# Low parts of the 42 projection weight units stored by the first block and loaded by the other three

## The reference

```
mod  = silu(c) @ W_ada + b_ada                    # shift, scale, gate for both halves
h    = rms_norm(x) * (1 + scale1) + shift1
proj = h @ W_in                                   # q,k,v | deltanet q,k,v | beta,decay | z | gate A | gate B
oA   = sliding_window_attention(...)              # window 128, sinks, QK norm, partial rope
oD   = gated_deltanet(causal_conv(qkv), ...)      # chunks, a triangular inverse per chunk
x    = x + gate1 * ((sigmoid(gA) * (oA @ Wb_A) + sigmoid(gB) * (oD @ Wb_B)) @ W_out)
x    = x + gate2 * swiglu(rms_norm(x) * (1 + scale2) + shift2)
```

## Time and profile before

| | |
|---|---|
| median of 3 runs | 2879.8 us (2879.57 to 2880.38) |
| the profiled execution's own time | 2879.23 us |
| its span | 2877.3 us |
| granted TensorE clock, mean | 0.995 |
| PE busy | 2830.7 us (98%) |
| DVE busy | 1815.7 us (63%) |
| ACT busy | 1239.3 us (43%) |
| DMA traffic | 523.51 MB, mean 182 GB/s |

### The profile page before, as it was taken

The page is one execution under the profiler, slowest core; times in us unless marked ns, Lnnn a source line. Parts: engine busy times, 40 slices in busy tenths (PEclk is TensorE's granted clock), DMA queues, the critical chain, the costliest instruction groups (busy, mean ns, idle before and its releaser), DMA issues.

```text
span 2877.3 us, 39886 instructions
## 1 busy us (share of the span) xinstructions
PE 2830.7 (98%) x14954; PEld 2331.7 (81%) x14954; DVE 1815.7 (63%) x3122; ACT 1239.3 (43%) x2232; POOL 133.3 (5%) x124
## 2 busy tenths in 40 slices
PE   8999999999999999999999999999999999999999
PEld 6887888977877888888889877788778888888887
DVE  5876576875687666658876666665757622223686
ACT  4654545554444333334445554365544311112343
POOL 0011000010020000000000110000100100000000
PEclk9999999999999999999999999999999999999999
DMA  7443354533448787886433334424243676777743
GB/s 289 157 147 107 121 165 132 187 95 115 142 165 311 291 296 291 298 332 207 140 116 111 120 94 136 154 82 156 78 140 121 218 242 232 245 245 264 299 136 102
DMA packets 222512, 523.51 MB, mean 182 GB/s; under 512 B 43249, under 2 KB 43505, under 8 KB 213361
## 3 DMA queue, kind: packets, MB, share of 16 engines
q1 hardware_dynamic: 173056, 423.39, 44.8%
q10 hardware_dynamic: 49264, 97.57, 8.9%
HBM read 362.03 MB, written 158.86 MB: 181 GB/s over the span
## 4 chain that ended last, share of the span: by engine, by line
PE 85%; DVE 7%; ACT 3%; DMA 2%; DVEq 2%; issue 1%; SPq 1%; POOL 0%; ACTq 0%
PE gb L2457 26%; PE mb L2501 22%; PE gb L2501 19%; PE gb L2882 5%; PE gb L2487 4%; PE mb L2726 2%; PE mb L2699 1%; PE mb L2721 1%; PE mb L2627 1%; ACT sc L1364 1%; DVE tmp_c L2068 1%; DVE w_lo L1616 1%; DVE inv_c L2071 1%; PE mb L2792 1%; DVE a_mx L2052 1%
## 5 line engine op out<-in xcount | busy, mean ns | idle before, releaser
L2457 PE MATMUL gb<-h_hi,w_hi 128*128 128x512 f32 x1024 | 408.2, 399 | 4.1 <-DVE w_lo L1616 3.5
L2457 PE MATMUL gb<-h_lo,w_hi 128*128 128x512 f32 x1024 | 406.2, 397 | 0.0
L2457 PE MATMUL gb<-h_hi,w_lo 128*128 128x512 f32 x1024 | 406.2, 397 | 0.0
L2501 PE MATMUL mb<-t_hi,fw_both 128*128 128x512 f32 x1056 | 349.9, 393 | 9.2 <-DVE t_lo L1794 5.1
L1616 DVE TENSOR_TENSOR w_lo<-w_raw,w_hi 128x1024 fp32r<-128x1024 f32 x216 | 262.7, 1219 | 80.1 <-ACT w_hi L1074 79.1
L1074 ACT ACTIVATE w_hi<-w_raw 128x1024 fp32r<-128x1024 f32 x216 | 227.9, 1055 | 87.7 <-PE gb L2882 40.9
L2501 PEld LDWEIGHTS mb<-t_hi,fw_both 128*128 128x128 f32 x1056 | 199.9, 189 | 54.5 <-DVE t_lo L1794 7.8
L2457 PEld LDWEIGHTS gb<-h_hi,w_hi 128*128 128x128 f32 x1024 | 192.9, 188 | 53.2 <-issue 7.3
L2457 PEld LDWEIGHTS gb<-h_lo,w_hi 128*128 128x128 f32 x1024 | 193.1, 189 | 42.8 <-issue 5.3
L2457 PEld LDWEIGHTS gb<-h_hi,w_lo 128*128 128x128 f32 x1024 | 192.9, 188 | 40.3
L2501 PE MATMUL gb<-td_hi,fw_both 128*128 128x512 f32 x704 | 219.7, 390 | 0.3 <-DVE td_lo L1783 0.2
(11 more groups left out here) (370 smaller groups left out, 5966.2 us busy)
## 6 DMA issues: line engine op xcount, KB each, us to landing
w_raw<-in_wstream SPq DMA_DIRECT2D x216, 512.0 KB, 3.6
scratch_parts<-fw_both ACTq DMA_DIRECT2D x154, 512.0 KB, 4.1
fw_both<-scratch_parts SPq DMA_DIRECT2D x154, 512.0 KB, 4.7
scratch_hid<-spill SPq DMA_DIRECT2D x22, 1792.0 KB, 7.4
td_raw<-scratch_hid SPq DMA_DIRECT2D x154, 256.0 KB, 3.0
ada_buf<-in_ada_w SPq DMA_DIRECT2D x24, 1024.0 KB, 7.7
w_raw<-in_wgate SPq DMA_DIRECT2D x34, 512.0 KB, 8.2
wq<-in_wdown SPq DMA_DIRECT2D x8, 1280.0 KB, 11.3
```

The costliest lines, as they stand in the source:

```text
L2457: last = pe.matmul(bank(j), w, r, start=(i == 0), stop=(i == n - 1))
L2501: done = pe.matmul(out, w, (lo if part == 1 else hi)[:, tile, :] if tile is not None else (lo if part == 1 else hi), start=(first and part ...
```

## The change

In block 0, units 12 to 53 are split as before, and ACT stores each one's `w_lo` to memory (`park_u`), two splits later. DVE waits for the store to land before it writes that slot's `w_lo` again. In blocks 1 to 3, DVE does not split these 42 units: ACT's `split` issues a DMA on its own queue that loads `w_lo` from memory into the slot, ahead of the high-part copy, and PE waits for the high part and for the landing. Units 0 to 11 of each block are split as before. SP's raw loads wait for the high part where the unit before in the slot is a kept one. Semaphores with an early use that is over are reused for the counts.

```diff
+def is_kept(g):
+    return g >= U_PER and g % U_PER >= U_AT
+def splits_to(g):
+    return sum(not is_kept(i) for i in range(g + 1))
+KEPT_PER_SLOT = (U_PER - U_AT) // RING
...
+    park_u = nc.dram_tensor("scratch_units", (U_PER - U_AT, P, UW), fp32, kind="Internal").ap()
...
             def load_unit(b, u):
-                sp.wait_ge(w_ready.sem, b * U_PER + (u + 1))
+                if is_kept(g - RING):
+                    sp.wait_ge(w_high.sem, w_high.at(0, g - RING + 1))
+                else:
+                    sp.wait_ge(w_ready.sem, w_ready.at(0, splits_to(g - RING)))
...
             def split(b, u):                      # ACT
+                unit_used(b, u - RING)
+                if is_kept(b * U_PER + u):
+                    if b == 1 and u == U_AT:
+                        for last in range(U_PER - RING, U_PER):
+                            act.wait_ge(*store_landed(last))
+                    act.dma_start(w_lo[s][:, :].bitcast(fp32), park_u[u - U_AT]).then_inc(kept_landed(b, u)[0], 16)
                 act.wait_ge(w_loaded[s], 16 * ((b * U_PER + u) // RING + 1))
-                unit_used(b, u - RING)
...
                 act.activation(w_hi[s][:, :], w_raw[s][:, :], ACT.Copy).then_inc(w_high.sem, 1)
+                if U_AT + 2 <= b * U_PER + u < U_PER + 2:
+                    store_unit(b * U_PER + u - 2)
+            def store_unit(g):
+                s = g % RING
+                act.wait_ge(w_ready.sem, w_ready.at(0, splits_to(g)))
+                act.dma_start(park_u[g - U_AT], w_lo[s][:, :].bitcast(fp32)).then_inc(unit_out[s].sem, 16)
...
             def split(b, u):                      # DVE
-                dve.wait_ge(w_high.sem, b * U_PER + (u + 1))
+                g = b * U_PER + u
+                if is_kept(g):
+                    return
+                dve.wait_ge(w_high.sem, w_high.at(0, g + 1))
+                if U_AT <= g - RING < U_PER:
+                    dve.wait_ge(*store_landed(g - RING))
...
+            def parts_there(b, u):                # PE
+                g = b * U_PER + u
+                if is_kept(g):
+                    pe.wait_ge(w_high.sem, w_high.at(0, g + 1))
+                    pe.wait_ge(*kept_landed(b, u))
+                else:
+                    pe.wait_ge(w_ready.sem, w_ready.at(0, splits_to(g)))
...
-                    pe.wait_ge(w_ready.sem, w_ready.at(b, u + 1))
+                    parts_there(b, u)
```

More of the change, by code:

```diff
@@ L152 @@
 LAST_USE, HALVES = last_uses()
+def is_kept(g):
[3 more added lines that the diff above has]
+KEPT_PER_SLOT = (U_PER - U_AT) // RING
+assert U_AT % RING == 0
 ADA_FIRST, ADA_TURNS = 4, 12
@@ L608, in layer_program, with kept_landed @@
     uses = [[n for n in range(N_GATE) if part_slot(1, n) == k] for k in range(PARTS)]
-    per_raw = [16 * (slots[k] + len(uses[k])) for k in range(6)]
-    f_loaded = [Signal(raw_in[k], per_raw[k]) for k in range(4)]
-    t_loaded = [Signal(raw_in[k], per_raw[k], gate_loads[k]) for k in range(6)]
-    parts_in = [Signal(raw_in[k], 0, gate_loads[k] + 16 * slots[k]) for k in range(6)]
+    unit_in = [KEPT_PER_SLOT * 16 if k >= 4 else 0 for k in range(6)]
+    per_raw = [16 * (slots[k] + len(uses[k])) + 2 * unit_in[k] for k in range(6)]
+    f_loaded = [Signal(raw_in[k], per_raw[k], unit_in[k]) for k in range(4)]
+    t_loaded = [Signal(raw_in[k], per_raw[k], unit_in[k] + gate_loads[k]) for k in range(6)]
+    parts_in = [Signal(raw_in[k], 0, 3 * unit_in[k] + gate_loads[k] + 16 * slots[k]) for k in range(6)]
+    def kept_landed(b, u):
+        k = (5, 4, None)[slot(b, u)]
+        n = (b - 1) * KEPT_PER_SLOT * 16 + 16 * ((u - U_AT) // RING + 1)
+        if k is None:
+            return sin_done, 2 + n
+        return raw_in[k], n + (gate_loads[k] + 16 * slots[k] if b >= 2 else 0)
     t_high, t_ready = sig("t_high", N_DOWN_STEPS), sig("t_ready", N_DOWN_STEPS)
@@ L634, in layer_program, with store_landed @@
     spilled = Signal(zeroed, 16 * NPAIR, 16 * 2 * NT)
+    unit_out = [Signal(sem, 0, 1) for sem in (c_silu, picks_set, picks_summed)]
     parts_out = [Signal(sem, 0, before) for sem, before in (
-        (c_silu, 1), (ada_kept, len(ADA_ROWS)), (nea_exp, 1), (picks_set, 1), (picks_summed, 1), (ada_rows, len(ADA_ROWS)))]
+        (c_silu, 1 + KEPT_PER_SLOT * 16), (ada_kept, len(ADA_ROWS)), (nea_exp, 1), (picks_set, 1 + KEPT_PER_SLOT * 16),
+        (picks_summed, 1 + KEPT_PER_SLOT * 16), (ada_rows, len(ADA_ROWS)))]
+    def store_landed(u):
+        return unit_out[u % RING].sem, unit_out[u % RING].at(0, 16 * ((u - U_AT) // RING + 1))
     def parts_count(n):
@@ L683, in load_unit @@
             def load_unit(b, u):
-                sp.wait_ge(w_ready.sem, b * U_PER + (u + 1))
-                s = slot(b, u)
+                g, s = b * U_PER + u, slot(b, u)
+                if is_kept(g - RING):
+                    sp.wait_ge(w_high.sem, w_high.at(0, g - RING + 1))
+                else:
+                    sp.wait_ge(w_ready.sem, w_ready.at(0, splits_to(g - RING)))
                 sp.dma_start(w_raw[s][:, :], wstream[UNITS[b * U_PER + u][0]]).then_inc(w_loaded[s], 16)
@@ L840, in _ @@
                             if v < 3:
-                                sp.wait_ge(w_ready.sem, w_ready.at(b, U_OUT + 6 + v))
+                                sp.wait_ge(w_high.sem, w_high.at(b, U_OUT + 6 + v))
                             elif v == 3:
```

## The result

The changed kernel takes 2887.5 us, the median of 19 runs (2878.9 to 2892.4), beside 2880.4 for the kernel before (19 runs, 2875.6 to 2884.0). The ratio is 1.0024, with a 95% interval of 1.0018 to 1.0031. The change makes the kernel slower by 0.24%; forecast was 0.12% faster, and the time lies 6 us above the range. Two later executions of the kernel before, of 3160.6 and 4003.8 us at clocks of 0.84 and 0.65, are left out of every ratio.

What follows compares the result with a forecast made beforehand. PE was taken as the bound, busy 2830.7 of 2877.3 us, so only its waits could shrink. 2879.23 - 6.8 (stops gone) + 2.3 (OUT+1) + 1.2 (block 0) = 2875.9; forecast for the median 2876.5 us, range 2870.5 to 2881.5.

Steps and rivals of the forecast that it cites:

- What bounds the kernel: Whole kernel: PE, busy 2830.7 of 2877.3 us, is the bound; only PE's waits in blocks 1 to 3 can be won.
- The inverse ends 3.5 us sooner: Blocks 1 to 3: three splits fewer on DVE end the inverse 3.5 us sooner and move the `lc_u` load forward.
- the one limit that I saw: Block 1: DVE's step at 621.27 needs ACT's copy, so it can start 1.15 us sooner instead of 1.22.
- I take about half, 1.0 us: Image DMAs: cost of a 512 KB unit load sharing from another queue, about half of 2.1 us.
- the margin of block 2: Worst block's `lc_u` stop: 3.5 - 1.9 - 0.6 = 1.0 us left before PE would wait for the image again.
- The images gain nothing: Rival, chance 0.22: unit loads and stores interleave with the image DMAs, 4.1 us less gain, 2880.6 us.
- Block 0, 1.2 us more: Block 0's `lc_u` stop: GATE+7's store stands with the image writes and adds 1.2 us, ends 0 and 4.2.
- OUT+1, 2.3 us more: Unit OUT+1, blocks 1 to 3: low part's load, issued after ACT's second square, lands 0.75 us later each, 2.3 in all.
- OUT+1 late: Rival, chance 0.11: OUT+1's low part lands at 8.3 us beside the raw load and `x`, costing 14 us: 2890.6.
- faster by over 0.2%: Outcome given 0.25: the rival that all stops of blocks 1 to 3 go (2868.9 us, 0.13) plus the forecast's lower edge.
- `w_lo` 1.7: Blocks 1 to 3, units GATE+8 and GATE+9: PE's stops for DVE's low part go, gain 1.7 us.
- `t_o` 0.6: PE's stop for `t_o` stays almost whole, since POOL's root limits it; gain 0.2 us a block, 0.6 in all.

Runs made afterwards that it cites:

- The second move: The change with only GATE+10's low-part load and GATE+8's store issued after the images' read back; 2874.0 us, 0.9979 of the kernel before.

## Why the prediction was wrong, step by step

- **What bounds the kernel**: right as far as it went. PE is busy 98% before and after, and the lighter DVE gained nothing as long as the images' way was not clear. But only PE's standing still was counted as what could be won or lost. The level of the clock behind a stop was no term, put at nothing without a reason: 2.7 us between the two traces, and about 5 of the 7 between the medians, by the estimate above.
- **The inverse ends 3.5 us sooner**: 2.76, 2.6 and 2.6. Two splits gone left DVE waiting for ACT again (0.24 and 0.40 us in the rows above) instead of the one limit that I saw.
- **"I take about half, 1.0 us"** for one neighbour, "which fits in the margin of block 2 and leaves something over": the failed term. The size was nearly right, 0.9 on the writes and 1.2 on the landing, but there are two neighbours, one on each half of the chain, and they add up to 2.1. The margin was too wide too, since the inverse gave 2.6 to 2.76, and PE comes 1.4 to 1.75 us sooner, not 0.6. Instead of 4.1 us gained, the stops in blocks 1 to 3 went from 4.5 to 7.1.
- **The images gain nothing**, the rival with 0.22, was the right mechanism and still too mild: it let the stops stay as they were and left out both PE's earlier arrival and the clock.
- **Block 0, 1.2 us more**: 2.0 measured (1.7 to 3.7), inside the ends of 0 and 4.2. That nothing else is waited for there was right.
- **OUT+1, 2.3 us more**: 1.1. The stops were to be 1.3, 1.0 and 1.0 us, 2.3 above those for `w_lo` that they replace; they are 0.7 three times, 2.1 in place of 1.0. The load landed in 3.25 us, not 3.6, and PE comes to it 0.4 us later behind ACT's second square than before:

```profile
775.14 0.33 ACTq L1108 DMA_DIRECT2D w_lo<-scratch_units  x1
...
778.48 0.47 PE L2517 MATMUL gb<-mg_hi,w_hi 128*128 128x512 f32 x1 [0.67 <-issue]
```

- **OUT+1 late**, the rival with 0.11, did not happen, although the load of `x` behind it took 12 us to land: it was issued 2.0 us after.
- **The chances**: 0.25 for "faster by over 0.2%" takes 0.12 from a forecast whose own range, 2873.5 to 2879, lies below 2874.0 for only half a us; that share is too large by the prediction's own numbers.
- **`w_lo` 1.7, `st_vr` 0.4, `t_o` 0.6, issues and waits 0, `a_mx` and `sc` 0**: 1.7 (the other 1.0 of the 2.7 is OUT+1's), 0.4, 0.4, and nothing new in the waits. Right.
- **The sum**: forecast -3.3 us. The stops of the two traces changed by +4.6 (`lc_u`: 2.6 in blocks 1 to 3, 2.0 in block 0) + 1.1 (OUT+1) - 1.7 - 0.4 - 0.4 = +3.2. That the traces differ by just about this, 3.1, is chance: 2.7 us lost behind the stops and 2.8 given back outside these rows cancel. Against the 2875.9 forecast for a profiled execution, 2882.3 is 6.4 too long, and the images' term alone is off by 6.7 (4.1 gained forecast, 2.6 lost). The other 4.6 of the 11 us between forecast and median lie between the change's profiled execution and its median, where the clock is lower (0.993 and 0.9921) and no trace was taken.

## What to carry over

A large transfer issued from another engine's queue is not off the path of small dependent transfers: find the chain write, read back, land, and place what is large before or behind it. Moving two loads in each of three blocks and two stores in the first by a few us turned 0.24% lost into 0.45% gained, with every byte kept. And a stop of a TensorE-bound kernel has to be priced with the work behind it: look at the granted clock in the windows after each stop of over a microsecond, or time a fixed piece of work behind it, and do so for every block, since one stop does not speak for the next. And put a stop's length beside the execution that it was read from, not beside the median of others.

## What was not expected of the hardware

- The granted clock can fall to half behind a stop of one to two us, and the work behind it then runs at 1.2 GHz without a pause. In the ten traces without added matmuls there are 40 stops for `lc_u`. Behind the 8 of under 1 us at most 0.1 us was lost. Behind the 19 of 1.07 to 1.97 us it was anything from 0 to 3.05, 1.5 in the mean. Behind the 13 of 2.09 to 3.7 us it was 2.9 to 4.1, but for the one of 2.35 us above with none.
- 24 short records of the identity inside a stop (2.84 us) kept the clock at 1.00 behind it, and fewer did so in blocks 1 and 3, whose stops are shorter; in block 2 of the same trace it fell all the same.
- Two queues share by bytes: one 512 KB load beside image transfers of 16 to 256 KB costs them 0.5 to 0.9 us on a chain of 6.1 to 6.6 and 1.2 to 1.3 on a landing of 3.6 to 3.7; at 128 KB and the same number of packets the cost was not to be seen in block 1 (in blocks 2 and 3 some 0.3 and 0.7 us of landing remained).
- The second move took 4.2 us from the stops and 13.5 from the time. The two numbers do not belong together: its profiled execution, 2878.9, is one of its slowest (2870.0 to 2879.4), and that of the change one of its fastest. As executions they are 3.4 us apart. Why executions of one kernel spread by up to 13 us, other than that the clock goes with it, stays open.
